# The last expert's down products by column blocks, with VectorE's row work reordered around them

## The reference, cut to what matters

```
def expert_block(args):
    xblk, e = args
    hdn = jax.nn.silu(xblk @ w_gate[e]) * (xblk @ w_up[e])
    return hdn @ w_down[e]
...
y = jax.ops.segment_sum(yb * row_w[:, None].astype(yb.dtype), row_tok, num_segments=T)
...
h = layer_norm(ALPHA * h + ffn, ln2_g[l], ln2_b[l])
```

## Time and profile before

| | us |
|---|---|
| median of 3 runs | 1932.79 |
| lowest and highest run | 1931.32 and 1936.6 |
| the profiled execution: its time | 1932.33 |
| the profiled execution: its span, first to last instruction | 1930.7 |
| PE busy in the span | 1837.2 (95%) |
| DVE busy | 1020.6 (53%) |
| ACT busy | 637.5 (33%) |
| POOL busy | 364.2 (19%) |
| hardware DMA queue, share of 16 engines | 64.7% |

### The profile page before, as it was taken

How to read it: one execution, slowest core, us unless ns; L and a number is a source line. 1 busy time by engine, 2 the same in 40 slices (tenths; PEclk the granted TensorE clock), 3 DMA queues, 4 the chain that set the end, 5 groups by cost and what they waited for, 6 DMA issues and landing times.

```text
span 1930.7 us, 25108 instructions
## 1 busy us (share of the span) xinstructions
PE 1837.2 (95%) x10358; PEld 1108.2 (57%) x10358; DVE 1020.6 (53%) x1713; ACT 637.5 (33%) x1052; POOL 364.2 (19%) x294
## 2 busy tenths in 40 slices
PE   5999999999999998999999999999999999999997
PEld 4778877887788776888843333333333333333332
DVE  6466655665652446433555554545545444454556
ACT  6323322332242556211423233232332323323234
POOL 0334323423333322445100000000000000000001
PEclk9999999999999998999999999999999999999998
DMA  7322222222222221553989999999999999999998
GB/s 265 85 66 67 66 67 66 66 66 67 66 75 66 66 66 44 196 154 123 359 326 421 426 427 426 426 428 425 427 426 427 425 428 426 426 427 426 425 427 334
DMA packets 147267, 503.39 MB, mean 261 GB/s; under 512 B 16680, under 2 KB 107048, under 8 KB 117840
## 3 DMA queue, kind: packets, MB, share of 16 engines
q1 hardware_dynamic: 142208, 492.70, 64.7%
q0 software_dynamic: 4944, 9.05, 1.2%
HBM read 496.88 MB, written 13.76 MB: 264 GB/s over the span
## 4 chain that ended last, share of the span: by engine, by line
PE 66%; DMA 21%; DVE 8%; ACT 2%; issue 2%; POOL 0%; SPq 0%; POOLq 0%; DVEq 0%; ACTq 0%
DMA ring<-in_w_up 21%; PE bank L2433 17%; PE bank L2010 10%; PE bank L2012 9%; PE bank L2011 9%; PE bank L2442 4%; PE bank L2406 4%; DVE half L1391 2%; PE bank L2157 1%; PE bank L2148 1%; DVE att L1597 1%; DVE sc L1592 1%; PE bank L2166 1%; DVE sc L1612 1%; PE bank L2238 1%
## 5 line engine op out<-in xcount | busy, mean ns | idle before, releaser
L2433 PE MATMUL bank<-ring,xbT 128*64 128x512 f32 x2048 | 469.4, 601 | 29.6 <-DMA ring<-in_w_up 29.0
L779 POOL TENSOR_TENSOR wlo<-raw,whi 128x512 fp32r<-128x512 f32 x232 | 312.5, 1378 | 526.1 <-ACT whi L906 371.6
L1844 DVE TENSOR_TENSOR r<-r,bank 128x512 f32<-128x512 f32 x464 | 287.5, 682 | 179.2 <-PE bank L2406 179.2
L2433 PEld LDWEIGHTS bank<-ring,xbT 128*64 128x64 f32 x2048 | 145.5, 137 | 305.7 <-issue 302.9
L2010 PE MATMUL bank<-hTh,wlo 128*128 128x512 f32 x704 | 298.6, 424 | 2.1 <-DVE hTl L1324 1.2
L2011 PE MATMUL bank<-hTl,whi 128*128 128x512 f32 x704 | 275.8, 392 | 0.0
L2012 PE MATMUL bank<-hTh,whi 128*128 128x512 f32 x704 | 275.7, 392 | 0.0
L2442 PE MATMUL bank<-ring,hidT 128*64 128x512 f32 x976 | 216.3, 595 | 0.5 <-ACT hidT L1198 0.5
L1849 DVE TENSOR_TENSOR yhl<-yw,yhl 64x512 fp32r<-64x512 f32 x120 | 82.8, 690 | 207.8 <-ACT yhl L1220 204.9
L825 POOL DMA_INDIRECT xb<-h_scr,idx_tok x32 | 31.8, 995 | 833.7 <-PE bank L2418 824.3
L906 ACT ACTIVATE whi<-raw 128x2048 fp32r<-128x2048 f32 x50 | 95.6, 1913 | 198.9 <-PE bank L2012 198.9
(11 more groups left out here) (362 smaller groups left out, 2042.5 us busy)
## 6 DMA issues: line engine op xcount, KB each, us to landing
ring<-in_w_down SPq DMA_DIRECT2D x61, 2048.0 KB, 23.3
ring<-in_w_gate SPq DMA_DIRECT2D x59, 2048.0 KB, 26.1
ring<-in_w_up SPq DMA_DIRECT2D x59, 2048.0 KB, 20.2
raw<-in_w_in SPq DMA_DIRECT2D x44, 1024.0 KB, 5.4
raw<-in_w_o SPq DMA_DIRECT2D x16, 1024.0 KB, 5.1
ring<-in_w_gate SPq DMA_DIRECT2D x10, 1024.0 KB, 12.8
ring<-in_w_up SPq DMA_DIRECT2D x10, 1024.0 KB
xt<-in_x SPq DMA_DIRECT2D x4, 1024.0 KB, 8.9
```

Source lines behind the costliest of these rows:

```text
L779: i = pool.tensor_tensor(wlo[sl][:, part, :], raw[sl][:, :].rearrange("p (k n) -> p k n", k=KD)[:, part, :], whi[sl][:, part, :].bitcast(F ...
L1844: dve.tensor_tensor(v, v, comb_bank(q, tt)[:, :], ALU.add).then_inc(comb_done, 1)
L2433: i = mm(GU[SLOTS * h:SLOTS * (h + 1), :], xT_[:, k, :], w[:, at_ * F:(at_ + 1) * F], start=k == 0, stop=k == KD - 1)
```

## The change

Four things are changed. First, the down products of the last expert are issued by column blocks: all four steps c for `DN[0]` (j = 0), and then all four for `DN[1]` (j = 1), where before each step c served both blocks. PE still waits for each piece of down weights ahead of the first use of it, which now falls in the pass for j = 0. Second, DVE does `full_rows(2)` ahead of `row_norm(0)`. Third, `row_sum(1)` is cut in two, each half with its block's `bn_stats`, and the two last passes of m = 0 (`row_out(0, j)`, taken out of `row_norm`) stand between and behind these halves. Fourth, the finished rows are counted by a new semaphore, `row_ready`, for which POOL waits, and `row_sum` takes the statistics of block 0 before the sum of block 1, so `ROW_DVE` is 9 and the number that PE waits for ahead of the last down products is 3.

```
-        ROW_DVE = 11
+        ROW_DVE = 9
...
-                pool.wait_ge(row_dve, ROW_DVE * (m + 1))
+                pool.wait_ge(row_ready, 2 * (m + 1))
...
-            def row_sum(m):
+            def row_sum(m, js=range(2)):
                 t = PLAIN + m
-                for j in range(2):
+                for j in js:
                     dve.wait_ge(rows_act, 2 * m + j + 2)
                     dve.wait_ge(w_used, 8 * t + 8 if t < E - 1 else 8 * t + 6 + 2 * j)
                     dve.scalar_tensor_tensor(out=rr_row[m][j][:, :], in0=DN[j][:, :], scalar=wts_all[:, ROWS[m]:ROWS[m] + 1],
                                              in1=rr_row[m][j][:, :], op0=ALU.mult, op1=ALU.add).then_inc(row_dve, 1)
-                for j in range(2):
-                    dve.wait_ge(row_dve, ROW_DVE * m + j + 1)
+                    dve.wait_ge(row_dve, ROW_DVE * m + 2 * j + 1)
                     dve.bn_stats(bns_r[:, m, j, :], rr_row[m][j][:, :]).then_inc(row_dve, 1)
+                if 1 not in js:
+                    return
                 dve.wait_ge(row_dve, ROW_DVE * m + 4)
                 dve.bn_aggr(mv_r[:, m, :], bns_r[:, m, :, :].rearrange("p a b -> p (a b)")).then_inc(row_dve, 1)
...
+            def row_out(m, j):
                 dve.wait_ge(row_dve, ROW_DVE * m + 9)
-                for j in range(2):
-                    dve.scalar_tensor_tensor(out=xb_half[m][:, j * F:(j + 1) * F], in0=rr_row[m][j][:, :], scalar=nm_r[:, m, 3:4],
-                                             in1=b2h[:, j, :], op0=ALU.mult, op1=ALU.add).then_inc(row_dve, 1)
+                dve.scalar_tensor_tensor(out=xb_half[m][:, j * F:(j + 1) * F], in0=rr_row[m][j][:, :], scalar=nm_r[:, m, 3:4],
+                                         in1=b2h[:, j, :], op0=ALU.mult, op1=ALU.add).then_inc(row_ready, 1)
...
             block_dve(E - 1)
+            full_rows(2)
             row_norm(0)
-            full_rows(2)
-            row_sum(1)
+            row_sum(1, [0])
+            row_out(0, 0)
+            row_sum(1, [1])
+            row_out(0, 1)
             row_norm(1)
+            for j in range(2):
+                row_out(1, j)
...
-            def last_down(c, w, at_):
-                for j in range(2):
-                    for h in range(2):
-                        n0 = (4 * at_ + 2 * h + j) * F
-                        i = mm(DN[j][SLOTS * h:SLOTS * (h + 1), :], hidT[:, c, :], w[:, n0:n0 + F],
-                               start=c == 0, stop=c == KF - 1)
-                        if c == KF - 1:
-                            i.then_inc(w_used, 1)
+            def last_down(c, w, at_, j):
+                for h in range(2):
+                    n0 = (4 * at_ + 2 * h + j) * F
+                    i = mm(DN[j][SLOTS * h:SLOTS * (h + 1), :], hidT[:, c, :], w[:, n0:n0 + F],
+                           start=c == 0, stop=c == KF - 1)
+                    if c == KF - 1:
+                        i.then_inc(w_used, 1)
...
-                    pe.wait_ge(row_dve, 2)
+                    pe.wait_ge(row_dve, 3)
...
                     else:
-                        last_down(c, ring[r_d], c % 2)
+                        last_down(c, ring[r_d], c % 2, 0)
+                if t == E - 1:
+                    for c in range(KF):
+                        last_down(c, ring[ring_of(t, 4 + c // 2)[0]], c % 2, 1)
```

More of the change, by code:

```diff
@@ L428, in build @@
         hot_done = sem("hot_done"); rows_ps = sem("rows_ps"); rows_act = sem("rows_act")
-        row_dve = sem("row_dve"); row_stored = sem("row_stored")
+        row_dve = sem("row_dve"); row_stored = sem("row_stored"); row_ready = sem("row_ready")
         gathered = [sem(f"gathered{i}") for i in range(2)]
```

## The result

The changed kernel takes 1936.46 us (median of 19 runs, 1933.82 to 1941.07) where the kernel before takes 1932.79 (19 runs, 1930.97 to 1937.87). The ratio is 1.0020, with an interval from 1.0013 to 1.0027: slower by 3.9 us, between 2.5 and 5.2. The forecast was no change, 1932.8 within 1930.9 to 1936.2. The runs of both kernels fall into two groups some 4 us apart (before: 12 runs from 1930.97 to 1932.96 and 7 from 1935.98 to 1937.87), so a single execution can stand 4 us high without the change.

What follows compares the result with a forecast made beforehand. Busy DMA engines bound the expert stage; only the tail, POOL's second scatter at 1926.20, counts. +0.92 and -0.51 end in the 0.62 slack: change 0.0, 1932.8 us, range 1930.9 to 1936.2.

Steps and rivals of the forecast that it cites:

- signs that the prediction named for being wrong: In the tail: first MOVE before 1922, no idle time in PE's group, or the granted clock falling inside it.
- the path of the forecast: Last expert's tail: down products +0.92, bn_aggr 0.41 later, L1978 ending at 1925.21, second scatter still at 1926.20.
- c = 3 waits for its weights: Last down products: PE idles about 0.9 after 12 instructions until the piece lands at 1914.3; products end 0.92 later.
- The landing of the stores: Last stores: issuing tile 2 earlier leaves the landing at 1924.0, as the slowest engines need 2.45 us a MB.
- The slack of 0.62: Before POOL's second scatter: rows of m = 1 may be ready until 1925.42 at no cost if stores land at 1924.0.
- part four: Counts in row_sum(0): hand-overs cost 0.1 to 0.2 ahead of L1872, where DVE idles for 1.43; effect nothing.
- part three: DVE's order: full_rows(2) and row_norm(0) hide in the wait for PE, 1.4 to spare; POOL's 6.59 at worst doubles; no effect.
- The rival for the slower side: Last down products: PE loses its clock in the new idle time before c = 3; +1.5, or +4.25 at the extreme; chance 0.12.

Runs made afterwards that it cites:

- old sums: Changed kernel with row_sum(0) back in its earlier order, both sums first and then both statistics (PE waits for 2 again), against the kernel before: ratio 0.9994, tail 26.2.
- POOL behind: Changed kernel with one more wait, so POOL's addition starts after full_rows(1), against the kernel before: ratio 0.9996, tail 26.2.
- new sums alone: Kernel before with only the order inside row_sum(0) changed to sum, statistics, sum, statistics (PE waits for 3): ratio 1.0023, tail 30.1.
- POOL first: Kernel before with one more wait, so DVE's full_rows(1) starts after POOL's addition: ratio 1.0029 against the kernel before, tail 29.9.
- mixed order: Changed kernel, POOL's addition after full_rows(1), PE taking c = 0 and 1 of block 1 before c = 3 of block 0: ratio 0.9997 against the kernel before.

## Why the prediction was wrong

Two of the signs that the prediction named for being wrong were there in the changed kernel: PE's last group has no idle time inside it, and the granted clock fell.

**What held.** With the order of the tie put right, the path of the forecast came out, but for `full_rows(2)` (below). The numbers stand in the runs with the old sums and with POOL behind: c = 3 waits for its weights after 12 instructions (0.78 and 0.77; forecast 0.9), the down products end 1.0 later (with the old sums 14.3 behind the start of the gate and up group, 13.4 before; forecast 0.92), `bn_aggr` starts 0.53 later (forecast 0.41), and the end doesn't move. The last pass of m = 1 ends only 0.14 later than before (20.43 against 20.29), because the two small matmuls ran at full clock and gave back 0.4; the forecast had them as they were, so that part is luck. The landing of the stores doesn't follow the issue of tile 2; it comes at 2.45 a MB behind the last down piece. That this is the rate of the slowest DMA engines is inferred from the DMA share of 0.20 in the earlier trace rows. The slack of 0.62 between the rows and the second scatter was real, and leaving one store out turned it into the gain that the sum gives.

**The step that failed** is the last of part four: "0.1 to 0.2 in all, ahead of L1872, before which DVE idles for 1.43 ... Nothing." The size was a little low, 0.25: from the first sum to `full_rows(0)` it was 2.92 before and is 3.17 after. Its cover, the idle time that was to hide it, was wrong. I looked for the next consumer of DVE's result, L1872, and found 1.43 of idle time ahead of it. Between the delay and that idle time lay a tie, `full_rows(1)` against POOL's addition, which DVE had won by 0.15. A delay above 0.15 reverses it (0.1 of the forecast 0.1 to 0.2 would not have, 0.2 would), and the loser pays what is left of the other's instruction: L1994 took 6.62 - 2.35 = 4.27 longer. Of the 1.43 of idle time 0.25 is used by the delay itself, and 0.26 because DVE's first row sum started 4.38 ahead of the gate and up group in place of 4.64. The 0.92 that is left comes off, and 3.35 remains; L1872 was 3.39 late.

**The same blind spot in part three.** There I asked what DVE does to POOL's addition ("Its 6.59 may grow by nothing or, at the worst, double") and not what the addition does to DVE. The rows held the answer. The addition started 0.15 behind `full_rows(1)`, and 6.59 is the rest of that pass, 2.2, plus 4.4. With DVE first, `full_rows(2)` did meet the addition, 4.44 in place of 2.34. The forecast gave `row_norm(0)` 1.4 to spare ahead of block 0; with the old sums it ended at 1915.54, 0.65 behind the end of block 0's products (1914.00 + 0.89), and nothing was to spare. It cost nothing only because the sum of block 1 had to wait for PE another 1.09.

The Trainium skill says (GPSIMD Engine Reference, key points) that GpSimd shares its SBUF interfaces with VectorE and that they contend when a DVE instruction has two SBUF inputs. The runs agree as to which instructions, L1992 being held and L1872, with one input in PSUM, not. The manner isn't in that sentence and is read from the runs: whole instructions exclude each other, 6.62 against 2.35. The price of 4.4 for a store of 1 MB, which the prediction takes from the Trainium skill (DMA: Bandwidth & Descriptors, anatomy of one DMA), is there a fit for DMAs issued by GpSimd; the stores here are issued by SP, and tile 2 landed between 4.1 and 10.0 after its issue.

**The rival for the slower side** named the right consequence and the wrong cause. PE lost its clock, but in the wait for DVE (4.26), not in the wait for weights, and that added 2.0. With a wait for weights of 0.6 to 0.8 the clock stayed full in five of five traces of this order of PE with DVE in time. In all three traces in which PE waited for about 4.2 ahead of the down products (the changed kernel, the new sums alone, and POOL first) it fell.

So the loss is: 0.25 of hand-overs in `row_sum(0)`, turned by the lost tie into 3.4 on PE's start, plus 2.0 of clock, less 0.85 for the sums and the small matmuls, less 0.6 of slack: 4.0.

**The resolution.** The prediction said that a measurement tells about 0.3% from no change and gave 0.94 to no change that can be told. With 19 runs of each kernel the interval is 0.07% to each side, and a loss of 0.2% is told.

**Still open.** In four of four traces of the mixed order the clock fell at the start of the down products, and in none of the six others in which DVE was in time, though PE's instructions and idle times ahead of that point are nearly the same (0.88 and 0.47 idle in all but one). Four of four against none of six is unlikely to be chance, and no run shows the cause; so a long wait for DVE isn't the only thing that brings the clock down. Without the fall the mixed order should make the rows of m = 1 ready about 0.5 earlier than before (an estimate, counted from the gate and up group: in the first trace the last pass ended at 21.44, the fall costs 8.78 - 7.09 = 1.69, and before it ended at 20.29); that wasn't seen. No version beat the kernel before: the five that repair the tie lie between 0.9994 and 0.9997, each with 1 inside its interval.

## What to carry to other kernels

Where two engines exclude each other, a delay is not covered by idle time further on: look for the ties between the delay and that idle time, and read who starts first and by how much. An instruction whose duration is the sum of its own and the rest of another's (6.59 = 2.2 + 4.4) marks such a tie in the kernel before. A tie won by 0.15 should be fixed by a semaphore, a reordering or a cut into short instructions before anything ahead of it is edited.

To learn what released an instruction, take the time of the register move behind its wait, not the name that the chain gives, and check a landing by the rate at which the queued megabytes land: here, stores issued earlier into a full queue landed no earlier.

## What the runs showed of the hardware

A DVE `scalar_tensor_tensor` with two full SBUF inputs and a POOL `tensor_tensor` did not run at the same time but for 0.2 us: 6.62 and 4.56 when POOL was first by 0.09, 2.35 and 6.59 when DVE was first by 0.15. A DVE instruction with one input in PSUM took 0.69 beside POOL. It is not the size that decides: in the kernel before, L1971 of m = 0 (128x512, both inputs in SBUF) started at 1911.19, while POOL's addition ran until 1911.80, and its two blocks took 1.81 in place of 1.41. The row was there to be read before the change, as a second sign of the exclusion.

The two small matmul groups of m = 1 ran at half clock in the kernel before (1.02 from the start of the first to the end of the second, after an idle time of 2.4) and at full clock in the changed kernel (0.62, after 1.9). But the kernel before with only the new sums had full clock there after 2.4 too, and of the four traces of the mixed order, all with 2.25, one had half clock. So the idle time alone doesn't tell which it will be, and about 0.4 hangs on it.
